# Moving GpSimd's gate sums ahead of a system load in the prompt's delta stage

## The reference, cut to what matters

```python
G = jnp.cumsum(gc, axis=-1)
dmask = jnp.exp(jnp.where(causal, G[..., :, None] - G[..., None, :], -jnp.inf))
lower = jnp.where(strict, jnp.einsum('...ik,...jk->...ij', kb, kc) * dmask, 0.0)
rhs = jnp.concatenate([vc * bc[..., None], kb * jnp.exp(G)[..., None]], axis=-1)
sol = lax.linalg.triangular_solve(jnp.eye(C) + lower, rhs, left_side=True, lower=True)
intra = jnp.einsum('...ik,...jk->...ij', qc, kc) * dmask
def step(S, xs):
    v_new = u_i - jnp.einsum('bhck,bhkv->bhcv', w_i, S)
    o = (q_i * exp(G_i)) @ S + a_i @ v_new
    S = S * exp(g_last) + (k_i * exp(g_last - G_i)).T @ v_new
```

## Time and profile before

| | us |
|---|---|
| median of 3 runs | 2520.29 (2519.49 to 2526.65) |
| profiled execution, own time | 2520.01 |
| its span, first to last instruction | 2518.1 |
| the stretch of `delta_prompt` in it | about 1651 to 1925 |
| PE, DVE, ACT, POOL busy in the span | 2357.5, 1602.9, 1126.1, 265.4 |

### The profile page before, as it was taken

The page is one execution under the profiler, slowest core; times in us unless marked ns, Lnnn a source line. Parts: engine busy times, 40 slices in busy tenths (PEclk is TensorE's granted clock), DMA queues, the critical chain, the costliest instruction groups (busy, mean ns, idle before and its releaser), DMA issues. The chain is left out here.

```text
span 2518.1 us, 44793 instructions
## 1 busy us (share of the span) xinstructions
PE 2357.5 (94%) x16770; PEld 2074.5 (82%) x16770; DVE 1602.9 (64%) x4082; ACT 1126.1 (45%) x2364; POOL 265.4 (11%) x458
## 2 busy tenths in 40 slices
PE   6999999999999999999999799679988699999998
PEld 3777788887999999999999677358877399999886
DVE  6767676553455677676444477478985577765565
ACT  4544454444323444444444467347775333332233
POOL 0000000000111111100000000223321001111000
PEclk8999999999999999999999899779997699999999
DMA  6222233333522322333332636765626545646442
GB/s 256 101 101 101 101 112 123 101 101 116 176 99 76 108 90 90 106 108 106 104 104 88 258 139 226 250 166 161 165 74 231 186 145 177 186 149 218 138 151 96
DMA packets 235373, 351.54 MB, mean 140 GB/s; under 512 B 47747, under 2 KB 171683, under 8 KB 229910
## 3 DMA queue, kind: packets, MB, share of 16 engines
q1 hardware_dynamic: 176386, 218.63, 28.1%
q0 software_dynamic: 33904, 117.83, 12.1%
q10 hardware_dynamic: 24868, 12.23, 1.7%
HBM read 241.23 MB, written 107.39 MB: 138 GB/s over the span
## 5 line engine op out<-in xcount | busy, mean ns | idle before, releaser
L305 PE MATMUL ps_f<-m_lo,w_hi 128*128 128x272 f32 (+1 forms) x2436 | 790.3, 324 | 12.2 <-DVE m_lo L615 5.5
L305 PE MATMUL ps_f<-m_hi,w_hi 128*128 128x272 f32 (+1 forms) x2436 | 794.0, 326 | 0.0
L305 PE MATMUL ps_f<-m_hi,w_lo 128*128 128x272 f32 (+1 forms) x2436 | 785.3, 322 | 0.0
L305 PEld LDWEIGHTS ps_f<-m_lo,w_hi 128*128 128x128 f32 x2436 | 459.1, 188 | 66.8 <-issue 31.3
L305 PEld LDWEIGHTS ps_f<-m_hi,w_lo 128*128 128x128 f32 x2436 | 460.0, 189 | 36.9
L305 PEld LDWEIGHTS ps_f<-m_hi,w_hi 128*128 128x128 f32 x2436 | 459.2, 188 | 33.9
L679 DVE TENSOR_TENSOR stage<-partial,ps_f 128x512 f32<-128x512 f32 (+2 forms) x348 | 171.4, 506 | 318.9 <-PE ps_f L305 307.4
L430 ACT ACTIVATE partial<-ps_f 128x272 f32<-128x272 f32 (+1 forms) x348 | 161.1, 463 | 392.6 <-PE ps_f L305 390.9
L392 ACT ACTIVATE w_hi<-w_raw 128x512 fp32r<-128x512 f32 x348 | 213.0, 625 | 204.3 <-PE ps_f L305 128.1
L586 DVE TENSOR_TENSOR w_lo<-w_raw,w_hi 128x512 fp32r<-128x512 f32 x348 | 239.1, 688 | 85.4 <-ACT w_hi L392 81.8
L65 PE MATMUL ps_fm<-u_lo,w_tail_hi 128*128 128x256 f32 (+1 forms) x768 | 223.8, 291 | 9.2 <-DVE u_lo L3040 8.6
(11 more groups left out here) (454 smaller groups left out, 3877.2 us busy)
## 6 DMA issues: line engine op xcount, KB each, us to landing
w_raw<-in_w_feat SPq DMA_DIRECT2D x58, 1024.0 KB, 5.8
gates<-scratch_g_d SPq DMA_DIRECT2D x56, 256.0 KB, 2.9
z_f<-scratch_z_d ACTq DMA_DIRECT2D x14, 768.0 KB, 4.7
scratch_conv_d<-conv POOLq DMA_DIRECT2D x18, 544.0 KB, 3.0
scratch_conv_d<-conv POOLq DMA_DIRECT2D x18, 512.0 KB, 2.9
kc<-in_k_cache SPq DMA_DIRECT2D x8, 1152.0 KB, 14.8
vc<-in_v_cache POOLq DMA_DIRECT2D x8, 1152.0 KB, 11.1
w_ada<-in_w_ada SPq DMA_DIRECT2D x8, 1024.0 KB, 14.1
```

The lines of the kernel that those rows point to most:

```text
L305: last = pe.matmul(out[:, 0:n], l[:, cols], r, start=start and k == 0 and nth == 0, stop=k == KH - 1 and nth == 2, skip_group_check=not start)
```

## The change

In passes in which there are both a pair to finish and a gate sum to make (`it` 0 to 4), each of the two gate sums now stands directly behind the stores of one chunk, and GpSimd's half of the system load stands behind both. In passes -2 and -1 (gate sums but no pair to finish) the order is the old one, and in passes 5 to 7 there are no gate sums.

```diff
                 if later(it + 2):
                     store_system(pool, 2 * (it + 2), 1)
+                if has(it) and has(it + 3):
+                    gates(2 * (it + 3))
                 if has(it):
                     store(2 * it)
                 if later(it + 2):
                     store_system(pool, 2 * (it + 2) + 1, 1)
+                if has(it) and has(it + 3):
+                    gates(2 * (it + 3) + 1)
+                if later(it + 2):
                     load_system(pool, it + 2, 1)
-                if has(it + 3):
+                if has(it + 3) and not has(it):
                     gates(2 * (it + 3)), gates(2 * (it + 3) + 1)
                 if has(it) and has(it + 1):
                     store(2 * it + 1)
```

## The result

The changed kernel took 2529.47 us (median of 13 runs, 2523.71 to 2534.64) and the kernel before, in the same series, 2519.04 us (13 runs, 2512.20 to 2526.65). The ratio is 1.0041, 95% interval 1.0033 to 1.0050: +10.3 us, slower by more than the 0.3% that a measurement can tell. In a second series it was 1.0031 (1.0020 to 1.0043), +7.8 us. The forecast had +5.2 us and a high bound of +8.1. The difference of two medians can lie up to 2 us beside it.

The account below looks back on a forecast made before the run. VectorE was taken to set the pace. Four passes at 1.3 us (5.2), plus 0.1 for pass 4, less 0.1 for a stall removed, gave +5.2 us: a median of 2525.5 us, range 2519.5 to 2530.

Parts of the forecast that it names:

- high bound: Passes 0 to 4: load moved by 1.82 us, landing in 5.1 (3.9 in pass 4), slow store in pass 2: +8.1 us.
- The chain: Passes 0 to 4: late stores, then a load landing late beside G rows, delay VectorE's elimination: +5.2 us, chance 0.60.
- the slack: TensorE's idle time before the next pass's first state update: hides up to 0.56 us of a late elimination start.
- The port rule: GpSimd's SBUF reads hold up only VectorE instructions with two SBUF inputs; relief in this stage at most 0.1 us.
- Rival (a): Passes 0 to 4: transfers fast enough to hide the later load, +0.7 us, 2521.0; chance 0.22.
- (b): VectorE's transposes also wait for the first chunk's gate sum, 1.3 us per pass: +6.4 us, 2526.7; chance 0.12.
- (c): Faster: pass 2's stall was paid in full and earlier loads clear the wire; 1.1 us at most, 2519.2; chance 0.06.
- The term of the stores: Passes 0 to 3: SyncE's system load follows the start of GpSimd's last store by 2.3 us.
- the reserve of 1.9 us: Pass 1: GpSimd's half of the load lands at 1742.9, 1.9 us before VectorE asks for it at 1744.80.
- The term of the landing: GpSimd's half of the load lands 5.1 us after issue in passes 0 to 3, 3.9 in pass 4.
- the stall that went: Pass 2: gate sums slowed VectorE's first product by 0.68 us; removing this gives back 0.1 us.
- the low bound: Load moves only by 1.82 us and lands as fast as before; only pass 2 loses time: +0.7 us.

Follow-up runs that it names:

- Run 3: The changed kernel, but SyncE waits in passes 0 to 4 for GpSimd's half to land before issuing G rows and key loads: 2522.53 us, ratio 1.0020.
- run 4: The changed kernel with the second chunk's gate sum back behind the system load, only the first chunk's sum moved: 2523.92 us, ratio 1.0028.
- run 1: The kernel before, with four GpSimd memsets (1.86 us) where the first gate sum would stand, both sums still behind the load: 2524.52 us, ratio 1.0029.
- run 2: The kernel before, with SyncE's key loads issued ahead of its G rows, directly behind the system loads of passes 0 to 3: 2521.96 us, ratio 1.0015.
- run 6: The kernel before, with both gate sums directly behind the second chunk's stores and both system-load halves issued by SyncE: 2520.52 us, ratio 0.9999.
- run 8: The changed kernel measured again, unaltered, on the chip of the other runs: 2528.14 us, ratio 1.0031.
- run 7: The changed kernel with 48 unread matmuls added in passes 1 to 4 where TensorE waited: 2528.74 us, ratio 1.0030.
- run 5: The changed kernel, but SyncE issues both halves of the system load back to back and GpSimd none: 2522.72 us, ratio 1.0010.
- Runs 9 and 10: Run 3's kernel with 24 and 60 unread one-column matmuls at the start of TensorE's row of the stage: 2528.03 us (1.0037) and 2547.89 us (1.0112).

## Why the prediction was right in its mechanism and wrong in its size

**Right.** The chain was as forecast: stores late by sum A, G rows 0.36 us behind SyncE's load, GpSimd's half slow in their company, the elimination late in all five passes, the slack gone. Run 3 takes the company away and run 4 a part of it, and the stretch of the passes falls from 11.4 to 1.9 and 6.9 us above the kernel before; run 1 has the delay without the company, and run 2 company without the delay, and each costs something. The port rule was right as well (a sum beside transposes cost nothing, 2.28 us), and so was the judgement that its relief is worth next to nothing (run 6). Rival (a) fell with the gaps and the landings, (b) with the transposes, (c) with the gaps and the slack that went.

**The term of the stores.** From the last store's start to SyncE's load I took 2.3 us for every pass. It was 3.83, 2.10, 2.66 and 4.26 in passes 0 to 3: 3.6 us more in all. The earlier trace rows had the case in view, the load of pass 2 after 4.06 us of idle time; I used it for the bounds alone, and for one pass. It is no property of a pass; two of the five passes drew it in both traces of the changed kernel, one to three of the five in the others. In the kernel before it fell into passes 2 and 5 and left no gap, since the reserve of 1.9 us covered it. Sum A had spent that reserve.

**The term of the landing.** I took 5.1 us from pass -1 and 3.9 in pass 4. It was 6.0, 6.5, 5.6 and 3.8, then 4.1: in passes 0 to 3 1.5 us more in all, but up to 1.4 in one. A single row was a thin base: pass -1 itself, whose order nothing changed, drew 4.8 to 6.3 us in the other traces that have it. Pass 3 is low in this trace and 5.2 in run 8.

**What adds up.** Gaps in passes 0 to 3 were 10.1 us, where 4 x 1.87 = 7.5 was forecast: 3.6 and 1.5 more from the two terms and 0.3 from the start of the product 0.08 us behind each landing; 0.3 less since GpSimd's load followed SyncE's by 0.16 us in pass 3; and 2.5 less since VectorE was itself later against the stores (from the last store's start to VectorE's readiness 6.37, 7.66, 6.16 and 6.35 us, where 6.02 was forecast).

**What was missing.** The prediction has no term for TensorE. Once VectorE waited, TensorE did too, and in this trace it came back at half clock; 1.64 of the 2.5 us given back above stand in pass 1, and 1.5 of those are the two longer waits for TensorE there (0.55, and 1.91 against 0.98). Gaps of 10.6 us in five passes and 0.7 in pass 5, less 1.7 for the slack of passes 0, 1 and 4 and 0.7 for the stall that went, and 2.8 for the longer waits, make 11.7; 11.4 was measured. What part of the 10.3 us is the clock is open: run 7 was to show it and didn't.

**The bounds and chances.** 2529.47 us lies within 2519.5 to 2530, but the difference of 10.3 us is above the high bound of 8.1, and slower by over 0.3% had 0.15. The high bound put both costs together but held a slow store in one pass, a landing of at most 5.1 us and no effect beyond VectorE. That the time is inside the range, by 0.5 us, is luck: the kernel before took 2519.04 us in this series, and from the 2520.29 that the forecast started from, +10.3 would be 2530.6. Two readings were off by little: the low bound leaves out the 0.4 us of pass 4 that the high bound counts, and SyncE's own half landed in 2.7 to 3.1 us in the kernel before, not 2.9 to 3.1.

## What to carry to other kernels

A reserve in front of the pacing engine isn't idle time to be filled. Here it paid for the slow draws of the transfers ahead of that engine, so size it against the worst of several passes and not against the median. When a wait is removed, list what other queues issue the moment it goes: here gate sums that ended earlier let 768 KB of G rows onto the wire beside the one load that was waited for. Where two halves of a load are both awaited, issue them back to back on one queue ahead of its bulk loads (runs 5 and 6), and on two queues only if the other one is quiet.

## What the runs showed of the hardware that was not expected

Two loads of 192 KB, issued 0.5 us apart, by SyncE and by GpSimd: with 384 KB loads directly behind on SyncE's queue, SyncE's half lands in about 3.0 us as without them, and GpSimd's in 5.6 to 6.8 in passes 0 to 2 of both traces of the changed kernel, where it is 2.9 without company. In pass 3 GpSimd's took 3.8 and 5.2. With both on SyncE's queue the second lands in 3.0 to 3.5 (run 6) and 2.9 to 3.8 (run 5). In these traces, what comes first on a queue keeps its time, and what stands on another queue shares with the bulk. The Trainium skill's page "DMA: Bandwidth & Descriptors", section "Queues, rings and completion order", says that a DMA engine goes round the queues that have work, packet by packet; the traces agree with that (6.5 us beside the G rows, 2.9 to 3.3 when they are held back in run 3), but the size varies: 2.9 to 4.9 us beside the key loads of run 2.

A 24 KB store of GpSimd's was slower where code was loaded. In the 12 traces there are 72 last system stores in passes 0 to 5. In the 33 with no transfer of instruction queue q8 starting in the 2.6 us behind the store's start, the wait from that start to the last landing was 2.0 to 2.6 us in 32 and 3.48 in one. In the 39 with one, it was 2.6 to 4.4, over 3.4 in 32. Runs 9 and 10 against run 3, and run 7 against the changed kernel, differ in TensorE's instructions alone, and the slow ones moved to other passes together with the transfers. That the transfer holds the store up, and does not merely fall in with it, is what this suggests; by which path is open. Each of these transfers is a single packet, 2 to 4% of the 16 engines' time in the 2.6 us (2.8% in the lines of run 9, so 1.2 us of one engine). So the 16 together are hardly short of bandwidth, but that a store waits for the one engine is not ruled out. GpSimd's 192 KB loads show the like. In passes 0 to 3 of the kernel before and of run 1, and 0 to 4 of runs 3, 9 and 10, SyncE issued nothing in the first 2.5 us behind its own half. Of these 23 landings, 21 took 2.8 to 3.3 us; the other two, 4.2 in pass 1 of run 1 and 4.3 in pass 2 of run 9, are the only ones in which a q8 transfer started in the 2 us behind the issue.

A granted clock of 0.50 came with 3.57 us of TensorE's idle time and lasted 6.8 us; a second one of 10.2 us began 16 us behind the last idle time above 1.4 us. In the seven traces in which TensorE was idle for at most 1.4 us at a time in the stretch of the passes (the kernel before, runs 2, 3, 5, 6, 9 and 10), the clock did not fall in it. In the other five, with idle times of 1.9 to 3.6 us, it did, but not always behind them: in run 8 it fell first at 1718.0, ahead of them all. What makes it fall here is open.
